# One VectorE operation for bias, negation and minimum in neighbourhood attention, with work moved out of the first attention heads

## The reference, cut to what matters

```python
def neighbourhood_attention(q, k, v, k_ctx, v_ctx, rpb):
    ...
    s_loc = jnp.einsum('brnqhd,brnkhd->bhrnqk', qg, kg).astype(jnp.float32) * scale + bias[None]
    s_loc = jnp.where(mask[None, None, None], s_loc, NEG_INF)
    s_ctx = jnp.einsum('brnqhd,bthd->bhrnqt', qg, k_ctx).astype(jnp.float32) * scale
    p = jax.nn.softmax(jnp.concatenate([s_loc, s_ctx], axis=-1), axis=-1).astype(v.dtype)
...
c_q = rms_norm(z[..., :OFF_CKV], mla_q_norm_g)            # MLA query latents
c_kv = rms_norm(z[..., OFF_CKV:OFF_KROPE], mla_kv_norm_g)
q_mla = (c_q @ w_q_up).reshape(b, s, MLA_HEADS, MLA_NOPE + MLA_ROPE)
gq = rms_norm(z[..., OFF_GQA:OFF_GK].reshape(b, s, GQA_HEADS, HEAD_DIM), gqa_q_norm_g)
k_lat, v_lat = mla_keys_values(c_kv, apply_rope(k_rope, cos_m, sin_m), w_kv_up[l])
```

## Time and profile before

| what | us |
|---|---|
| median of 3 runs | 1824.57 |
| profiled execution, its own time | 1820.75 |
| span of that execution (first to last instruction) | 1818.9 |
| busy PE / DVE / ACT / POOL | 1710.9 / 1163.4 / 692.3 / 213.4 |
| attention, layer 0: last z eviction to wait for w_out | about 160 to 390 |
| attention, layer 1 | about 1047 to 1265 |

### The profile page before, as it was taken

One profiled execution on the slowest core, in us unless ns is written; L12 is line 12 of the kernel. 1 busy time (PEld: TensorE's weight loads), 2 busy tenths in 40 slices (PEclk: granted clock), 3 DMA queues, 4 the chain that ended last, 5 costly groups with the idle time before them and its releaser, 6 DMA issues.

```text
span 1818.9 us, 28617 instructions
## 1 busy us (share of the span) xinstructions
PE 1710.9 (94%) x11442; PEld 1655.1 (91%) x11442; DVE 1163.4 (64%) x2215; ACT 692.3 (38%) x1359; POOL 213.4 (12%) x314
## 2 busy tenths in 40 slices
PE   6899889889999999999999988988999999999997
PEld 6898777779899999999999977877999999999997
DVE  5996867858767777666652577786364444444444
ACT  2434756753522222222244376676252222222222
POOL 0003543310000000000010272332000000000001
PEclk9999999999999999999999999999999999999999
DMA  9462000053434433333122010002312222222201
GB/s 353 163 217 66 10 1 3 1 162 116 162 140 143 152 121 127 127 127 127 50 90 83 10 44 1 1 1 74 89 53 87 70 92 92 69 69 69 69 23 58
DMA packets 105526, 159.80 MB, mean 88 GB/s; under 512 B 5024, under 2 KB 83680, under 8 KB 105184
## 3 DMA queue, kind: packets, MB, share of 16 engines
q1 hardware_dynamic: 102800, 153.26, 25.2%
q10 hardware_dynamic: 2160, 3.23, 0.5%
q0 software_dynamic: 480, 2.19, 0.4%
HBM read 155.09 MB, written 3.57 MB: 87 GB/s over the span
## 4 chain that ended last, share of the span: by engine, by line
PE 82%; DVE 9%; ACT 3%; DMA 2%; issue 2%; POOL 1%; SPq 0%; POOLq 0%; DVEq 0%; ACTq 0%
PE ps L636 25%; PE ps L638 24%; PE ps L637 24%; PE ps L887 2%; PE ps L644 2%; DVE ps L1364 1%; DVE negmax L1596 1%; PE ps L860 1%; DVE hT L1349 1%; DMA ada_n<-in_w_ada_first 1%; PE ps L862 1%; DMA wo_raw<-in_w_out 1%; DVE K L1349 1%; PE ps L716 1%; DVE pT L1349 1%
## 5 line engine op out<-in xcount | busy, mean ns | idle before, releaser
L636 PE MATMUL ps<-hT,gw 128*128 128x320 f32 x1408 | 435.2, 309 | 2.2 <-DVE hT L1349 2.2
L637 PE MATMUL ps<-hT,gw 128*128 128x320 f32 x1408 | 435.1, 309 | 0.0
L638 PE MATMUL ps<-hT,gw 128*128 128x320 f32 x1408 | 435.1, 309 | 0.0
L1432 DVE SCALAR_TENSOR_TENSOR x<-ps,mod,x 128x320 f32<-128x320 f32 (+2 forms) x576 | 211.7, 432 | 96.7 <-PE ps L638 93.5
L636 PEld LDWEIGHTS ps<-hT,gw 128*128 128x128 f32 x1408 | 264.3, 188 | 2.9 <-issue 2.9
L637 PEld LDWEIGHTS ps<-hT,gw 128*128 128x128 f32 x1408 | 264.3, 188 | 0.0
L638 PEld LDWEIGHTS ps<-hT,gw 128*128 128x128 f32 x1408 | 264.3, 188 | 0.0
L1682 DVE TENSOR_TENSOR mm<-sl,ps 128x320 f32<-128x320 f32 x88 | 42.7, 487 | 316.8 <-issue 185.4
L636 PE MATMUL ps<-act,dw 128*128 128x320 f32 x704 | 218.3, 310 | 2.7 <-DVE act L1349 2.7
L637 PE MATMUL ps<-act,dw 128*128 128x320 f32 x704 | 218.2, 310 | 0.0
L638 PE MATMUL ps<-act,dw 128*128 128x320 f32 x704 | 218.1, 310 | 0.0
(11 more groups left out here) (218 smaller groups left out, 3571.3 us busy)
## 6 DMA issues: line engine op xcount, KB each, us to landing
ada_w<-in_w_adaT SPq DMA_DIRECT2D x48, 512.0 KB, 5.9
gw_raw<-in_w_gate SPq DMA_DIRECT2D x22, 1024.0 KB, 5.5
gw_raw<-in_w_up SPq DMA_DIRECT2D x22, 1024.0 KB, 8.0
dw_raw<-in_w_down SPq DMA_DIRECT2D x22, 1024.0 KB, 4.9
ada_wf<-in_w_adaT SPq DMA_DIRECT2D x34, 512.0 KB, 6.8
wi_raw<-in_w_in SPq DMA_DIRECT2D x12, 1216.0 KB, 6.7
wo_raw<-in_w_out SPq DMA_DIRECT2D x16, 512.0 KB, 5.0
ada_wq<-in_w_adaT SPq DMA_DIRECT2D x10, 512.0 KB, 4.1
```

The lines of the kernel that those rows point to most:

```text
L636: pe.matmul(dst, lh, rh, start=start, stop=False, skip_group_check=True)
L637: pe.matmul(dst, lh, rl, start=False, stop=False, skip_group_check=True)
L638: return pe.matmul(dst, ll, rh, start=False, stop=stop, skip_group_check=True)
L1432: i = ve.scalar_tensor_tensor(out=x[:, o, c0:c1], in0=ps[:, banks + hf_, s0:s0 + c1 - c0], scalar=mod[:, l, part * KD + o, q:q + 1], in1=x ...
```

## The change

- **Fused bias and maximum.** `tensor_tensor_reduce` adds the bias tile to all scores of the unit, multiplies by -1 and accumulates the minimum into `negmax`, which replaces the add, the wait and the reduction. The bias tiles get 128 more columns of zeros for the cached keys (`BIAS_COLS`, two zero blocks shared between neighbours; so for units 1 and 3 the cached keys stand first). The scores are then negated in PSUM, and the exponential uses scale -1.
- **Layer 0's GQA sums of squares** run beside the projection, as in layer 1; a dummy exponential behind the square roots (`warm[:, 3:4]`, both layers) loads ACT's table there.
- **Key rotation** (`KR`) and the **zeros of K** go to POOL ahead of attention; GQA's memsets stay on DVE.
- **Order in the first slots:** `CL` to slots 1 and 2, `QU` to slots 3 to 6 and 8, 9 ahead of the transposes, with the evictions as `QE` half a slot later; queries wait for two latent tiles, not three. The first filler matmuls follow three units, not two; those of NA start at unit 10, not 9.

```diff
@@ schedule()
-    spread([("CL", 0), ("CL", 1), ("CL", 2)], 0, 2)
-    for n in range(8):
-        extra[2 * (2 + n // 2) + 1].append(("QU", n))
-    extra[13].append(("CT", 3))
-    extra[15].append(("QU", 8))
-    extra[17].append(("QU", 9))
-    spread([("KR", t) for t in range(4)], 1, 4)
+    extra[3] += [("CL", 0), ("CL", 1)]
+    extra[5] += [("CL", 2)]
+    for n in range(0, 8, 2):
+        extra[6 + n] = [("QU", n), ("QU", n + 1)] + extra[6 + n]
+        extra[7 + n] += [("QE", n), ("QE", n + 1)]
+    extra[14] = [("CT", 3)] + extra[14]
+    for n in range(8, 10):
+        extra[2 * n] = [("QU", n)] + extra[2 * n]
+        extra[2 * n + 1].append(("QE", n))
     spread([("QR", t) for t in range(4)], 5, 8)
-    spread([("GS", t) for t in range(NT)] + [("GR",)], 8, 16)
@@ tensor, queries and scores
-                pe.wait_ge(cT_ready, l * 4 + (3 if t < 4 else 4))
+                pe.wait_ge(cT_ready, l * 4 + (2 if t < 4 else 4))
-                        if u < 2:
+                        if u < 3:
                             keep_busy(4, 3)
-                        if u == 9:
+                        if u == 10:
                             pe.wait_ge(qm_done, l * 2 * NT + 2 * NT)
-                        if kind == "na" and u >= 9:
+                        if kind == "na" and u >= 10:
                             keep_busy(1, 2)
@@ scalar
-                        if c == 4 and t == (NT - 1 if (l == 0) else 1):
+                        if c == 4 and t == (NT - 1 if l == 0 else 1):
                             sc.wait_ge(cstat_ms, 2 * l + 1)
                             sc.activation(stat[:, :, 0:2], stat[:, :, 0:2], ACT.Sqrt).then_inc(cstat_rms, 1)
-                            if not (l == 0):
-                                g_rms()
+                            g_rms()
+                            sc.activation(warm[:, 3:4], eps[:], ACT.Exp)
...
-                        if l:
-                            sc.wait_ge(z_done, l * IC * NT + G_CHUNKS * NT)
-                            for t in range(NT):
-                                g_square(t, rstd[:, 0:512])
+                        sc.wait_ge(z_done, l * IC * NT + G_CHUNKS * NT)
+                        for t in range(NT):
+                            g_square(t, rstd[:, 0:512])
@@ vector
-                if kind == "gqa" or kind == "na" and h < 2:
+                if kind == "na" and h == 0:
+                    ve.wait_ge(key_zeros, l + 1)
+                if kind == "gqa":
                     ve.memset(K[64:P, kb, 1, :].bitcast(F32), 0.0)
...
-                            ve.tensor_tensor(ps[:, bk, 0:w], ps[:, bk, 0:w], bias_h[:, g % 2, NA_OFF[i]:NA_OFF[i] + w],
-                                             ALU.add).then_inc(biased, 1)
-                            ve.wait_ge(biased, l * 16 + 4 * g + i + 1)
-                            src = ps[:, bk, 0:w + P]
+                            ve.tensor_tensor_reduce(out=ps[:, bk, 0:w], in0=ps[:, bk, 0:w],
+                                                    in1=bias_h[:, g % 2, UNIT_OFF[i]:UNIT_OFF[i] + w], scale=-1.0, scalar=HUGE,
+                                                    op0=ALU.add, op1=ALU.min, accum_out=negmax[:, u:u + 1]).then_inc(max_ready, 1)
@@ gpsimd, ahead of the schedule
+                po.wait_ge(z_done, l * IC * NT + 2 * NT)
+                for t in range(4):
+                    if t:
+                        po.wait_ge(q_roped, l * 8 + t)
+                    rotate(l * OWN + 3 * t, 1, 32, z[:, t, OFF_KR:OFF_G].unsqueeze(1), ...)
+                po.wait_ge(wi_ready, l * IC + IC)
+                settled(po, passed_po)
+                po.memset(K[:, :, 1, :].bitcast(F32), 0.0).then_inc(key_zeros, 1)
```

More of the change, by code:

```diff
@@ L78 @@
 NA_COLS = 1280
+BIAS_COLS = NA_COLS + 2 * P
+BIAS_OFF = [0, 384, 768, 1280]
+ZERO_OFF = [256, 1152]
+UNIT_OFF = [0, 256, 768, 1152]
+CACHE_FIRST = [False, True, False, True]
+HUGE = 3.0e38
 def na_range(m):
@@ L847, in _ @@
                             w = (m1 - m0 + 1) * P
-                            parts = [(bk, 0, w, m0 * P), (bk, w, P, LAT)]
+                            parts = [(bk, 0, P, LAT), (bk, P, w, m0 * P)] if CACHE_FIRST[i] else [(bk, 0, w, m0 * P), (bk, w, P, LAT)]
                         else:
@@ L883, in _ @@
                                 m0, m1 = NA_M[i]
-                                pos = (m1 - m0 + 1 if mt == 4 else mt - m0) * P
+                                if CACHE_FIRST[i]:
+                                    pos = (0 if mt == 4 else 1 + mt - m0) * P
+                                else:
+                                    pos = (m1 - m0 + 1 if mt == 4 else mt - m0) * P
                             else:
@@ L1158, in exponentials @@
                     dst = probs[:, g % 2, i, :].rearrange("p (a b) -> p a b", a=2)
-                sc.activation(dst, src, ACT.Exp, bias=negmax[:, u:u + 1], accum_out=rsum[:, u:u + 1]).then_inc(exp_done, 1)
+                sign = -1.0 if kind == "na" and i < 4 else 1.0
+                sc.activation(dst, src, ACT.Exp, scale=sign, bias=negmax[:, u:u + 1], accum_out=rsum[:, u:u + 1]).then_inc(exp_done, 1)
             for k in range(KD):
@@ L1268, in _ @@
                         sc.activation(ckvT[:, 0, LAT:640], kc_mla[:], ACT.Copy).then_inc(wqk_hi, 1)
[L1269 to L1272, removed]
                     elif s[0] == "V":
@@ L1282, in _ @@
                         i.then_inc(v_hi, 1)
-                sc.activation(warm[:], eps[:], ACT.Sqrt)
+                sc.activation(warm[:, 0:1], eps[:], ACT.Sqrt)
                 for o in range(KD):
@@ L1308, in _ @@
                 modulated(l, 1)
-                sc.activation(warm[:], eps[:], ACT.Silu)
+                sc.activation(warm[:, 0:1], eps[:], ACT.Silu)
                 def ffn_block(b, last):
@@ L1548, in _ @@
                         ve.tensor_scalar(stat[:, :, 1:2], stat[:, :, 1:2], 1.0 / P, EPS, ALU.mult, ALU.add).then_inc(cstat_ms, 1)
[L1549 to L1552, removed]
+                        for t in range(NT):
+                            g_sum(t, rstd[:, 0:512])
+                        g_mean()
                     if l == 0:
@@ L1622, in _ @@
                         lo(ckvT[:, 1, LAT:640], kc_mla[:], ckvT[:, 0, LAT:640]).then_inc(wkv_ready, 1)
-                    elif s[0] == "GS" and l == 0:
-                        g_sum(s[1], ztmp[:])
-                    elif s[0] == "GR" and l == 0:
-                        g_mean()
                     elif s[0] == "V":
@@ L1774, in _ @@
                 settled(po, passed_po)
+                z0 = bias_h[:, 0, ZERO_OFF[0]:ZERO_OFF[0] + P]
+                po.memset(bass.AP(tensor=z0.tensor, offset=z0.offset, ap=[list(z0.ap[0]), [BIAS_COLS, 2],
+                                                                          [ZERO_OFF[1] - ZERO_OFF[0], 2], [1, P]]), 0.0)
                 value_zeros(0)
-                turned = 0
                 for s in SCHED:
```

50 lines of the change are left out of this document (23 added, 27 removed).

## The result

The changed kernel takes 1812.35 us (median of 14 runs, 1805.86 to 1820.35) against 1825.11 us for the kernel before (14 runs on the same chip, 1820.60 to 1830.80): a ratio of 0.9927, 95% interval 0.9916 to 0.9939. The profiled execution took 1806.87 us with a span of 1805.1, against 1820.75 and 1818.9 before: 13.8 us less span, at a granted clock of 0.990 against 0.986. It is the third shortest of its 14; the difference of the medians is 12.8 us.

The account below looks back on a forecast made before the run. The NA stage was taken as bound by the round trip between in-order engines, DVE busiest. Gains 6.6 + 1.4 + 0.6 + 4.2 + 3.0 - 0.8 = 15.0 us gave 1805.8 profiled, 1807 median (1801 to 1812; wider 1795 to 1818).

Parts of the forecast that it names:

- half rate: Rival, chance 0.05: the fused DVE operation runs at half throughput and gains nothing; 8.4 us gain in all, 1812 to 1813.
- fused operation: NA units: one DVE operation replaces add and maximum, saving 6.7 us a layer of DVE time; 6.6 us gain in all.
- zeros of K: DVE's second memset, behind unit 0's maximum without idle time, leaves the path: 0.7 us a layer, 1.4 us in all.
- sums and tables, layer 0: Layer 0's attention loses two table loads, 4.2 us gain; the first exponential's load goes in both layers, 0.6 us.
- order: First attention slots: moved latents, queries and evictions shorten waits of PE and ACT; 1.5 us a layer, 3.0 us gain.
- fillers: Extra NA matmuls: three more after unit 2, two fewer at unit 9, a net -0.8 us in both layers.
- Several passes: Rival, chance 0.05: the fused DVE operation takes several passes and DVE becomes the bound; some +15 us, 1836.
- Half of it passes: Of the 6.7 us a layer DVE saves in NA, half shortens the path: 3.3 us a layer, 6.6 us.
- Everything passes: Rival, chance 0.12: DVE's whole 6.7 us and 3 us from reordering come through a layer; 24.8 us gain, 1796.
- The path moves: Rival, chance 0.18: DVE's gain in NA is given back by waits for ACT and PE; 4.8 us stay, 1816.
- The projection's slack: End of layer 0's projection: ACT's held-back eviction has 1.2 us to spare, no stall; cost 0, else 1 to 2 us.
- Layer 0 against layer 1: NA start to second pair's end: layer 0 takes 5.1 us more, mostly table loads; 4.2 us gain, about 0.9 kept.

## Why the prediction was right, step by step

1807 us was forecast, inside 1801 to 1812; the median is 1812.35, just above that band and inside the wider range of 1795 to 1818. The sum for the profiled execution was 15.0 us, and 13.9 came (1806.87 against 1805.8). The median missed by 5 us because of the step from the sum to the median: it was to lie 0 to 4 us above, taken as about 1, although before it lay 3.8 (in the end 4.4) above the profiled execution; it lies 5.5 above it. The number by itself fits the rival "half rate" (1812 to 1813) better than the forecast. It is the row of the fused operation, and not the time, that rules this rival out. That the sum came within 1 us is partly luck: the stages gained 1.2 us more than foretold, in part by dips that were in no term, and the second and third pairs of layer 0 gained less.

| term | foretold | measured |
|---|---|---|
| fused operation | 6.6 | 5.1 to 6.7 alone, a dip a layer in it; 5.1 (stages), 3.8 (time) in the changed kernel |
| zeros of K | 1.4 | 0.1 at the memset in layer 0; 2.8 to 4.4 with the rotations, cause open |
| sums and tables, layer 0 | 4.2 + 0.6 | 3.9 to 4.7 alone; 3.1 in the second pair, some 0.9 of it a dip; 1.6 lost in the third, a dip |
| order | 3.0 | 2.0 alone; 3.5 to 4.1 in the changed kernel |
| fillers | -0.8 | within what can be told |
| both NA stages | 10.8 | 12.0 |

- *The fused operation.* 0.80 us was taken for 512 columns with the read; the rows add up to 0.687 + 0.134, and from the start of the one at 167.79 to the end of its read at 168.53 it is 0.74. "Several passes" and "half rate" are out. The rule of the Trainium skill (Vector Engine (DVE) Microarchitecture Reference, Points that are easy to get wrong) speaks of two SBUF sources that are not bf16. This operation has one source in PSUM and one in SBUF, and it ran at the speed of the one-source maximum. "Half of it passes" was near: 5.1 us of the 13.4 that DVE was to save, or of the 15.4 that it was less busy in the two stages. "Everything passes" failed, as layer 0's sums had suggested.
- *The path moves.* It did in part: the rest of DVE's saving is idle time of DVE, such as the 1.42 us for ACT's half of K. But the NA stages kept their 12.0 us.
- *Zeros of K* is the step that failed. "No idle time behind the memset" was true and not enough: the next step's other producer, ACT, ended at the same moment. I had read when DVE was free and not when ACT's half was done.
- *The projection's slack* held: no gap on PE, one table load, DVE free at 160.17 before the NA heads. The loads in the middle of attention are gone; in layer 1 the one load stands at 1020.15. The 0.6 us for the first exponential's load were not measured by themselves.
- *Layer 0 against layer 1.* From the first unit to the end of the second pair it is 74.57 us against 72.82, so 1.75 us remain of 5.1, against the 1 foretold. The term of 4.2 us was read from a difference that holds the dip at 232: in the trace of the zeros alone, which has the sums in their old place and no dip there, the second pair lasts 24.90 us and not 25.78. By these two traces, both at full clock there, the sums and loads cost 24.90 - 22.66 = 2.2 us. The lost 1.6 us in the third pair were in no term: a dip, which the kernel before lacks in its profiled execution and all four of its variants have.
- *The order.* The mechanism named (PE's wait behind DVE, 2.10 and 2.71 us) fell to 1.86 and 1.84 us by the order alone and to 0.72 and 0.73 in the changed kernel. Its size was left to a guess, since I priced only the wait, and not the slow clock behind it.

The four parts alone add up to 0.89% (0.28 + 0.26 + 0.11 + 0.24), together they give 0.73%. The difference is smaller than what the intervals leave open (added as independent errors, some 0.28%), so the runs do not show an overlap. The traces suggest one: the dip at 188 is missing with the fused operation, with the order and with the zeros, the one at 1075 with the fused operation, the sums and the zeros. No run has two parts together. What decides a dip stays open too: the same code behind the same wait shows it in one execution and not in another (1092 to 1104 above), and the kernel before has none behind its 2.69 us at 262.07.

## What to carry to other kernels

When a step is taken off an engine, look for when the next step's other inputs are done, not only whether its engine was idle: here that made 0.7 us into 0.1. In a stage bound by round trips, between a third and two fifths of the time saved on the busiest engine came through (5.1 of 15.4 or of 13.4 us). Read the granted clock beside every window of the stage, before a difference between two stages or two traces is given to the work in them; and fill PE's own waits with matmuls that nobody reads: in the one gap followed here they cost nothing and gave 1.5 us, and the matmuls behind the later NA units could come out again.

## What the runs showed of the hardware

- TensorE's granted clock falls in single short stretches. In the one at 252.39 the score matmuls of 320 columns take 0.47 us and from 255.86 on 0.32 and less. The falls stand behind waits of PE, those at 188, 252 and 1075 behind one of 2.1 to 2.7 us, those at 172, 232, 1058 and 1092 behind two or three of 0.5 to 1.5 us, and the priced ones cost 0.95 to 1.6 us each. The same waits also pass without a fall: 2.69 us at 262.07 in the kernel before, 2.09 and 2.11 us with the fused operation alone, 2.48 us in layer 1 with the sums alone. Up to 370 us and from 1030 to 1240 us the profiled execution of before has five of them (172, 188, 232, 1058, 1075), that of the changed kernel one (252).
- The spread of equal runs goes with the clock: spans of the changed kernel and their mean clocks go together, 1804.1 us at 0.992, 1805.1 at 0.990, 1808.9 at 0.988, 1812.9 at 0.985, 1818.5 at 0.982. The 0.010 between the ends would be some 18 us of 1805 by my estimate, and 14.4 are there.
- `tensor_tensor_reduce` with two inputs, an output in PSUM and an accumulated minimum costs 1.02 ns a column ((687 - 556) / 128), as the plain maximum does, and 134 ns for the read of its accumulator.
- In the key rotations on POOL one operation on 128x32 took 2.58 us (103.84), while DVE ran conditioning products and a weight split, where the same operation had taken 286 ns in the mean before; over all eight it is 934 ns. PE shows no gap in layer 0's projection, so it cost nothing there.

```profile
103.84 2.58 POOL L1737 TENSOR_TENSOR z<-z,rstd 128x32 f32<-128x32 f32 x1
```
